# A two-layer encoder on one core: attention steps in another order, a rotation shared between VectorE and GpSimd, the low-part matmuls last, and a start with three panels

## The reference

```
h   = rmsnorm(x);  proj = h @ w_in            # 2048 x 4352, columns for A, B, C
A: 8 heads, attention with clipped relative bias, QK-norm
B: 16 query heads on 2 KV heads, window of 2 chunks, sinks, QK-norm + rotary
C: 4 heads, two softmax maps, p0 - lam * p1, QK-norm + rotary, then rmsnorm
x   = x + concat(A, B, C) @ w_out             # 2048 x 2048
x   = x + relu(rmsnorm(x) @ w_up)^2 @ w_down  # 2048 x 8192, 8192 x 2048
```

## Time and profile before

| | |
|---|---|
| median of 3 runs | 2122.57 us (2121.98 to 2126.64) |
| the profiled execution | 2122.87 us, of which the span of instructions is 2121.0 us |
| TensorE matmuls busy | 98% of the span |
| VectorE, ScalarE, GpSimd busy | 60%, 48%, 9% |

### The profile page before, as it was taken

How to read it: one execution, slowest core, us unless ns; L and a number is a source line. 1 busy time by engine, 2 the same in 40 slices (tenths; PEclk the granted TensorE clock), 3 DMA queues, 4 the chain that set the end, 5 groups by cost and what they waited for, 6 DMA issues and landing times.

```text
span 2121.0 us, 26490 instructions
## 1 busy us (share of the span) xinstructions
PE 2084.7 (98%) x10598; PEld 1738.0 (82%) x10598; DVE 1274.8 (60%) x1635; ACT 1010.3 (48%) x1353; POOL 197.6 (9%) x205
## 2 busy tenths in 40 slices
PE   7999999999999999999999999999999999999999
PEld 6877778888888888888878777788888888888887
DVE  6667556565565555556666675556655555565666
ACT  5456654443443444344445576544434434443444
POOL 2544120000000000000033431000000000000000
PEclk9999999999999999999999999999999999999999
DMA  8566786666666666666666568766666666666664
GB/s 262 163 183 169 178 230 178 189 189 195 190 189 191 191 189 195 190 189 190 185 175 181 159 177 204 202 182 187 194 192 189 190 196 190 189 190 194 189 192 149
DMA packets 209387, 400.70 MB, mean 189 GB/s; under 512 B 14862, under 2 KB 21872, under 8 KB 209264
## 3 DMA queue, kind: packets, MB, share of 16 engines
q1 hardware_dynamic: 203856, 381.85, 60.8%
q0 software_dynamic: 4608, 16.78, 4.3%
q10 hardware_dynamic: 800, 0.37, 0.1%
HBM read 380.05 MB, written 2.12 MB: 180 GB/s over the span
## 4 chain that ended last, share of the span: by engine, by line
PE 94%; DVE 2%; ACT 2%; issue 1%; DMA 1%; SPq 0%; DVEq 0%; POOL 0%; ACTq 0%; POOLq 0%
PE psum L475 22%; PE psum L439 19%; PE psum L441 19%; PE psum L440 18%; PE psum L478 12%; PE psum L485 1%; PE psum L545 1%; ACT w_hi L637 1%; DMA x<-in_x_dram 1%; PE psum L532 1%; PE psum L530 1%; DVE w_lo L806 1%; PE psum L571 0%; DVE probs L952 0%; DMA w_lo<-raw_ring 0%
## 5 line engine op out<-in xcount | busy, mean ns | idle before, releaser
L806 DVE TENSOR_TENSOR w_lo<-raw_ring,w_hi 128x1024 fp32r<-128x1024 f32 (+1 forms) x692 | 854.4, 1235 | 764.5 <-ACT w_hi L637 764.2
L637 ACT CAST w_hi<-raw_ring 128x1024 fp32r<-128x1024 f32 (+1 forms) x724 | 753.8, 1041 | 1006.5 <-PE psum L441 611.6
L475 PE MATMUL psum<-xt,w_hi 128*128 128x512 f32 x2048 | 512.9, 392 | 0.0
L439 PE MATMUL psum<-w_hi,ht_hi 128*128 128x512 f32 x1280 | 502.8, 393 | 1.3 <-DMA w_lo<-raw_ring 1.2
L441 PE MATMUL psum<-w_hi,ht_lo 128*128 128x512 f32 x1280 | 498.6, 390 | 0.0
L440 PE MATMUL psum<-w_lo,ht_hi 128*128 128x512 f32 x1280 | 498.3, 389 | 0.0
L475 PEld LDWEIGHTS psum<-xt,w_hi 128*128 128x128 f32 x2048 | 368.8, 189 | 66.3
L478 PEld LDWEIGHTS psum<-xt,w_lo 128*128 128x128 f32 x2048 | 279.4, 190 | 20.0
L478 PE MATMUL psum<-xt,w_lo 128*128 128x256 f32 x2048 | 285.6, 282 | 0.0
L439 PEld LDWEIGHTS psum<-w_hi,ht_hi 128*128 128x128 f32 x1280 | 240.3, 188 | 53.3 <-issue 5.1
L441 PEld LDWEIGHTS psum<-w_hi,ht_lo 128*128 128x128 f32 x1280 | 240.2, 188 | 50.8
(11 more groups left out here) (125 smaller groups left out, 1070.8 us busy)
## 6 DMA issues: line engine op xcount, KB each, us to landing
raw_ring<-in_w_up_dram SPq DMA_DIRECT2D x256, 512.0 KB, 3.7
raw_ring<-in_w_down_dram SPq DMA_DIRECT2D x256, 512.0 KB, 3.7
raw_ring<-in_w_in_dram SPq DMA_DIRECT2D x132, 512.0 KB, 4.2
raw_ring<-in_w_out_dram SPq DMA_DIRECT2D x64, 512.0 KB, 4.8
w_lo<-raw_ring POOLq DMA_DIRECT2D x32, 512.0 KB, 5.5
raw_ring<-in_w_in_dram SPq DMA_DIRECT2D x16, 256.0 KB, 2.8
x<-in_x_dram SPq DMA_DIRECT2D x4, 512.0 KB, 10.1
out_dram<-x SPq DMA_DIRECT2D x4, 512.0 KB, 3.9
```

What stands on the lines that cost most here:

```text
L439: pe.matmul(out_ap, t_hi, m_hi, start=start, stop=False, skip_group_check=True)
L475: pe.matmul(bank[:, f, :], w_hi[:, w, j, f * P:(f + 1) * P], both, start=kt == 0, stop=False, skip_group_check=True)
L637: act.copy(w_hi[:, u % AHEAD, :, 0:cols], raw_ring[:, u % RAWS, :, 0:cols]).then_inc(hi_ready, 1)
L806: dve.tensor_tensor(w_lo[:, u % AHEAD, :, 0:cols], raw_ring[:, u % RAWS, :, 0:cols], w_hi[:, u % AHEAD, :, 0:cols].bitcast(F32), ALU.subtr ...
```

## The change

What it does, part by part:

1. **Order in a rows unit.** The four tiles' hi·hi and lo·hi matmuls come first (8), then the four hi·lo ones. The wait for `w_hi` stands ahead of the 8, the wait for `w_lo` ahead of the last 4.
2. **Attention steps.** Both exponentials of a pair are in one step of ScalarE (s + 1), behind the split. `COMBINE` and `WEIGHT` are one step earlier on VectorE. `NORM_AT` has a table of its own: every head norm is one to four steps ahead of its old place. `POST_C` 0 goes from the front of step 46 to its end.
3. **Rotation.** Row tile 1 of Cq and Ck is rotated by VectorE (`rope`), right after their sums.
4. **Adding DMAs.** `SUMMED_UNITS` ends at 81: 14 units.
5. **x2 panels** (of the MLP's input) are two steps apart instead of one.
6. **Start.** Three panels before unit 0, panels 3 and 4 behind units 0 and 1; 10 and 14 further transposes of the identity (`warm`) into a PSUM bank that nobody reads. ScalarE issues its eight small DMAs after the second panel and its squares; SP issues the tables in step 3, and the parameters are worked out in steps 5 to 7.
7. **End.** In the last layer the unused panels, loads and splits are left out. The last unit does row tile 0 first, and each row tile is added and stored by itself.

```diff
-SUMMED_UNITS = list(range(55, 87, 2))
+SUMMED_UNITS = list(range(55, 83, 2))
-EXPS = {s + 1 + m: 2 * n + m for s, n in PAIR_AT.items() for m in range(2)}
-COMBINE = {s + 4: n for s, n in PAIR_AT.items() if n < 4}
-WEIGHT = {s + 3: n for s, n in PAIR_AT.items() if n >= 4}
+EXPS = {s + 1: n for s, n in PAIR_AT.items()}
+COMBINE = {s + 3: n for s, n in PAIR_AT.items() if n < 4}
+WEIGHT = {s + 2: n for s, n in PAIR_AT.items() if n >= 4}
-        T_USE[OUT_LAST[_c] + 2 + _n + (1 if _c == 1 else 0)] = ("x2", 2 * _c + _n)
+        T_USE[OUT_LAST[_c] + 2 + 2 * _n + (3 if _c == 1 else 0)] = ("x2", 2 * _c + _n)
-NORM_AT = {s: use[1:] for s, use in T_USE.items() if use[0] == "qk"}
+NORM_AT = {11: (0, 1), 13: (0, 0), 20: (1, 1), 22: (1, 0), 38: (3, 0), 45: (4, 0), 46: (4, 1), 52: (5, 0), 54: (5, 1),
+           58: (6, 0), 60: (6, 1), 66: (7, 0), 68: (7, 1)}
...
@@ block.tensor, rows_unit
-                unit_is_split(pl, u)
-                for j, kt in enumerate(kts):
-                    for r in range(RT):
-                        mm = three_passes(bank[r][:, 0:cols], src[0][:, kt, r * P:(r + 1) * P],
...
+                pe.wait_ge(hi_ready, pl.unit(u + 1))
+                final = pl.l == DEPTH - 1 and u == UNITS - 1
+                tiles = [(j, kt, r) for j, kt in enumerate(kts) for r in range(RT)]
+                for group in [[t for t in tiles if t[2] == r] for r in range(RT)] if final else [tiles]:
+                    for j, kt, r in group:
+                        for n, t in enumerate(src):
+                            pe.matmul(bank[r][:, 0:cols], t[:, kt, r * P:(r + 1) * P], w_hi[:, slot, j, 0:cols],
+                                      start=first and j == 0 and n == 0, stop=False, skip_group_check=True)
+                    unit_is_split(pl, u)
+                    for j, kt, r in group:
+                        mm = pe.matmul(bank[r][:, 0:cols], src[0][:, kt, r * P:(r + 1) * P], w_lo[:, slot, j, 0:cols],
+                                       start=False, stop=last and j == 1, skip_group_check=True)
+                    if final and r == 0:
+                        mm.then_inc(row0_done, 1)
                 mm.then_inc(unit_done, 1)
...
@@ block.tensor, start
+                if pl.l == 0 and s < 2:
+                    first_panel(3 + s)
...
-            for k in range(PANELS_BEFORE):
-                pe.wait_ge(x_loaded[k // 2], 16)
-                transposes(x_panel(k), start_banks[k])
+            warm(10)
+            first_panel(0)
+            first_panel(1)
+            warm(14)
+            first_panel(2)
...
@@ block.scalar
-                if s in EXPS:
-                    exponentials(pl, EXPS[s])
                 split_hi(pl, u, PROJ[u // UPC][2] if u < PU else CW)
...
+                if s in EXPS:
+                    for m in range(2):
+                        exponentials(pl, 2 * EXPS[s] + m)
...
+                if n == 1:
+                    load_small()
...
@@ block.vector
+            def rope(pl, c):
+                t, heads, half, r = c, 8, HD // 2, 1
...
+                dve.wait_ge(rope_ready, pl.l + 1)
+                dve.wait_ge(summed, pl.at(len(QK), QK.index(c) + 1))
+                dve.tensor_tensor(b_r[:, :, lo], a_r[:, :, hi], table(rope_s, 0, half), ALU.mult)
+                link(dve.tensor_tensor(b_r[:, :, hi], a_r[:, :, lo], table(rope_s, half, half), ALU.mult))
+                link(dve.tensor_tensor(a_r, a_r, table(rope_c, 0, HD), ALU.mult))
+                dve.tensor_tensor(a_r[:, :, lo], a_r[:, :, lo], b_r[:, :, lo], ALU.subtract)
+                link(dve.tensor_tensor(a_r[:, :, hi], a_r[:, :, hi], b_r[:, :, hi], ALU.add))
...
-                if s in POST_C:
-                    post_c(pl, POST_C[s])
                 if s in WEIGHT:
                     weight(pl, WEIGHT[s])
+                if s in NORM_AT:
+                    head_norm(pl, *NORM_AT[s])
+                if s in POST_C and POST_C[s]:
+                    post_c(pl, POST_C[s])
                 if s in STATS_AT:
                     head_sums(pl, STATS_AT[s])
-                if s in NORM_AT:
-                    head_norm(pl, *NORM_AT[s])
+                    if STATS_AT[s] < 2:
+                        rope(pl, STATS_AT[s])
...
@@ block.gpsimd, rotation
-                for r in range(RT):
+                for r in range(1 if c < 2 else RT):
```

More of the change, by code:

```diff
@@ L224, in encoder @@
         roped = sem("roped")
+        rope_ready = sem("rope_ready")
         normed = sem("normed")
@@ L361, in mix @@
                 u = s + FIRST_LOADS
+                if pl.l == 0 and s == 3:
+                    load_tables()
                 if u < PU:
@@ L986, in mix @@
                     split_lo(pl, u, PROJ[u // UPC][2] if u < PU else CW)
-                if s == 0:
+                if pl.l == 0 and s == 5:
+                    tables()
+                if pl.l == 0 and s == 6:
+                    parameters()
+                if s == (7 if pl.l == 0 else 0):
                     dve.tensor_copy(cur[:, :], par[:, pl.l, :]).then_inc(cur_ready, 1)
@@ L1002, in mix @@
                     add_out(pl, s)
+                if s in POST_C and not POST_C[s]:
+                    post_c(pl, POST_C[s])
             def mlp(pl, s, part, buf, c, k, n):
-                if s - 1 in PANEL_NUMBER:
+                more = pl.l < DEPTH - 1 or s + AHEAD < UNITS
+                if s - 1 in PANEL_NUMBER and used(pl, s - 1):
                     panel_lo(pl, s - 1)
-                if s < UNITS - 1:
+                if s < UNITS - 1 and more:
                     split_lo(pl, s + AHEAD)
@@ L1014, in mlp @@
                         dve.wait_ge(rstd_ready, pl.at(2, 2))
-                    dve.wait_ge(unit_done, pl.unit(s + 1 + AHEAD))
+                    final = pl.l == DEPTH - 1 and s == UNITS - 1
+                    if not final:
+                        dve.wait_ge(unit_done, pl.unit(s + 1 + AHEAD))
                     dve.wait_ge(evicted[p], pl.evictions(n))
@@ L1018, in mlp @@
                         v = x[:, r, (c % 4) * CW:(c % 4 + 1) * CW]
+                        if final and r == 0:
+                            dve.wait_ge(row0_done, 1)
+                        if final and r == 1:
+                            last.then_inc(row0_out, 1)
+                            dve.wait_ge(unit_done, pl.unit(s + 1 + AHEAD))
                         last = dve.scalar_tensor_tensor(v, acc[:, 2 * p + r, :], rstd[:, 1, r:r + 1], v, ALU.mult, ALU.add)
                     last.then_inc(evicted[p], 1)
-                if s == UNITS - 1:
+                if s == UNITS - 1 and more:
                     split_lo(pl, s + AHEAD)
```

168 lines of the change are left out of this document (95 added, 73 removed).

## The result

| | before | after |
|---|---|---|
| median, runs on the same chip | 2124.61 us (4 runs) | 2095.73 us (4 runs, 2095.67 to 2096.25) |
| profiled execution; span | 2122.87; 2121.0 us | 2095.73; 2093.6 us |

The ratio is 0.9866 with a 95% interval of [0.9854, 0.9878]: faster, by 28.9 us on the medians, where 19.8 had been forecast from the terms.

The account below looks back on a forecast made before the run. TensorE, busy 98% of the span, was taken as the bound, so only its waits and needless work count. Attention 17.5, start -1.7 and end 4.0 sum to 19.8 us off 2122.87: 2103 us, range 2096 to 2114.

Parts of the forecast that it names:

- What bounds the kernel: Whole kernel: TensorE's matmuls are busy 98% of the span, so only its waits or needless work can be won.
- Start: First units up to the PSUM bank behind unit 3: bank empty at 32.5 us, 0.9 later; 1.7 us lost in all.
- The landing of the second unit: Second weight unit's load at the start: lands at 14.21 us, less 1.25 for ScalarE's 0.37 MB no longer ahead.
- The issues: ScalarE's eight small DMA issues at the start: now stand in its chain ahead of the bank and add 4.2 us.
- The clock: TensorE after the idle time at the start: granted clock lost in one of two cases, half of 1.7 us, 0.8.
- The rival for this outcome: Start is won: issues cost little or loads come sooner, no clock lost; 2.5 instead of -1.7, 2095 to 2099 us; 12%.
- The rule on issuing engines: DMAs of different issuers share 16 engines: ScalarE's issues at 16 us compete with weight loads and worsen the chain; unpriced.
- Attention: TensorE's 13 waits for norms, weights, copies and an adding DMA: 19.5 us gross, 17.5 taken, ends 9 and 20.5.
- The x2 panels: Panels of the MLP's input, two steps apart: no wait of any size there, 0 us, ends -1 and +1.
- The rule on the shared port pair: VectorE and GpSimd block each other at SBUF: their rotations would push each other back, losing part of the gain.
- the rival that had them collide: Waits half replaced: VectorE and GpSimd collide at Cq and Ck, or issues take 8 us; 2107 to 2111 us; 18%.
- Order in the unit, end: Rows units' same 12 matmuls reordered: 0 us, upper end 17; kernel's end, panels 2.8, last addition 0.7, DMA 0.5: 4.0 won.

## Why the prediction was right, and where it was off

The direction and the mechanism were right, and the size was 7.6 us of span too small, in two terms: 3.8 us in the start and 3.8 in attention. With that the time fell just below the stated range.

**What bounds the kernel: right.** The gains that the unit starts place are idle time, lost clock or needless work of TensorE. In the MLP stages, two thirds of the span, only 0.2 us were won, at panels.

**Start: the mis-sized term, and of the wrong sign.** Forecast -1.7, measured +2.1, from one trace of each kernel, with a scatter of up to 1.4. Forecast was a bank empty at 14.21 - 1.25 + 8.0 + 0.6 + 4.2 + 6.74 = 32.5; it is empty at 28.00. Its pieces:
- The landing of the second unit, 14.21 - 1.25 = 12.96: it was cast at 9.96. This is the step that failed. I counted the bytes of ScalarE's queue only, and those I had about right (at least 1.1 us measured). The change also put SP's own tables, gains and norm2_g behind the weight loads, and of them I said nothing but that they are issued in step 3. Measured by putting them back: 2.5 us for that landing, 2.71 us of waiting for the fifth unit's load, and 4.0 us at unit 5.
- The issues: 4.2 forecast, 2.9 in the chain. They take 3.45 us (11.67 to 15.12), of which 0.6 beside the squares; the third panel's cast starts 5.21 us after the second unit's instead of 2.33. That they stand in the chain was right: that cast waits 2.79 us.
- The rest of the chain, 8.0 + 0.6 + 6.74 = 15.34, was 18.04 - 2.9 = 15.1: right. But the 2 us left out of it were called "DMA and table work", and 1.43 of them are a wait for the fifth unit's load in the earlier trace rows. That it went was not argued; it went with SP's new order, and with the old one it is back, at 2.71 us.
- The clock: the forecast took half of 1.7 us. It was lost in full in the profiled execution, 4.06 - 2.72 = 1.3 us.

The rival for this outcome was named, at 12%, with its price of 2.5. Its "the loads come sooner" is what happened; its "no clock is lost" is not. "Against: the last took 1.03" looked at the issues, and the issues were not what decided. Of the signs named for a right forecast, one failed for the same reason: the transposes behind unit 3 came at 28.09, not at 31 to 34 us.

**The rule on issuing engines: borne out, and I weighed it at the wrong place.** In 8 to 12 us the weight loads run at these rates (last column GB/s), first the changed kernel, then the one with ScalarE's DMAs at the start:

```profile
8.00:12.00 4.00, 4.00 (x22) 3.86 (x21) 2.99 (x4) 3.97 (x7) 0.00 (x0) 1.00 1.06 394
```

```profile
8.00:12.00 4.00, 4.00 (x25) 3.35 (x24) 3.13 (x5) 2.39 (x3) 0.00 (x0) 1.00 0.96 268
```

ScalarE's queue in those 4 us is 430 packets with 0.19 MB, and takes 33.8% of the DMA engines' time, with 18% of the bytes (the loads move 0.88 MB beside it):

```profile
q10 hardware_dynamic: 430, 0.19, 33.8%
```

By the Trainium skill's "DMA: Bandwidth & Descriptors", section "Issuing engines are not separate DMA queues", DMAs of different issuers run on the same 16 engines and interleave. These rows agree: another issuer's DMAs take time from the loads, and by more than their bytes. The prediction applied this to the issues at 16 us, as a loss. In the changed kernel no cast up to the bank waits for a load, so no loss is seen there; what is seen is the gain of what no longer stands at 8 us.

**Attention: right in kind, 3.8 us too low, panels included.** The 17.5 came from 13 waits, 19.5 gross less 2.0 left. The unit starts give:
- Gross 23.9 us, the sum of all gains over single units. I had left out the small rows of the waits (L880 1.0, L917 0.5, L922 0.4, in 6 waits), 1.9 us of idle time and about 3 with what a wait costs on top.
- A wait costs more than 0.16 us beside its idle time: with 1.42, 2.00, 0.70 and 2.34 us idle, 1.64, 2.21, 0.94 and 2.55 us were won. It is 0.22 in front of transposes.
- The clock was worth 1.4 us, not 1.7, and is kept now.
- New waits take 4.2 us, where I had 2.0 for all that is left: two of 1.45 and one of 0.74, all for L982. The cause of the first two is not what I named as a danger (the combined exponentials) but the norm ahead of the copy; the third is a split slowed beside GpSimd's tables.
- The x2 panels, priced at 0 with +1 as an end, won 0.7 us in each layer, and the next layer's x panels 0.2. Without these panels attention won about 19.6, inside the ends of 9 and 20.5.

The prediction's "this, not the order, is what makes Cq's first norm early enough", on the 6.1 us less of GpSimd, is not shown: undoing both costs 6.2 us, but GpSimd was done in time in either kernel. "The wait for an adding DMA was at unit 85 of the second layer, which VectorE now splits" did not hold as a cause: given back to the adding DMA, that unit waits no more, since its w_lo matmuls come last.

**The rule on the shared port pair: a mixed answer, as before.** GpSimd and VectorE at Cq, in the changed kernel:

```profile
47.53 2.95 POOL L1209 TENSOR_TENSOR small<-small 128x16 f32<-128x16 f32 x1
50.46 1.00 POOL L1232 TENSOR_TENSOR head_sq<-head_in,rope_s 128x256 f32<-128x256 f32 x1
...
56.48 1.72 POOL L1236 TENSOR_TENSOR head_in<-head_in,head_sq 128x256 f32<-128x256 f32 x1
```

```profile
48.11 0.69 DVE L925 TENSOR_TENSOR head_in<-head_in,rope_c 128x512 f32<-128x512 f32 x1
...
54.14 1.77 DVE L945 TENSOR_TENSOR head_in<-head_in,small 128x512 f32<-128x512 f32 x1
```

VectorE's whole rotation, 47.26 to 49.60, lies beside the reciprocal root of GpSimd, and neither is slowed (2.95 against 2.91 us in the earlier trace rows; 0.69 for 512 columns, where an undisturbed norm takes 0.68). VectorE's norm beside GpSimd's rotation takes 1.77 instead of 0.68 us, and that rotation 7.7 us, where with splits alone beside it it took 6.1 before and 7.1 in the run with GpSimd's rotation whole. By the Trainium skill's "SBUF — State Buffer", section "SBUF: two separate sides", each should block the other for whole instructions: the rotation's rows agree, and so does the split of 3.00 us beside GpSimd's tables, the root's don't. The two rotations do not meet, because the root stands ahead of GpSimd's (49.60 and 50.46 us); the rival that had them collide (18%) did not come.

**Order in the unit, end: right.** 0 and 0.0; 4.0 and 2.6 + 1.4 = 4.0. The w_up row's 0.230 belongs to its narrow matmuls, as said.

## What to carry to other kernels

When DMAs are moved, write down for every queue what they no longer stand in front of; a few hundred small packets can delay a neighbouring 512 KB load more than their bytes say. Before pricing a removed wait, add up all rows of waits, the small ones too, and for each operation moved ahead on an engine name the one that now stands behind it: here Bq1's norm, for which nobody had waited, went ahead of a copy and cost 1.6 us a layer. When an engine gets less to do, ask what it now does earlier, and beside whom: here GpSimd's tables moved beside a split and cost 0.9 us. And look at the chain in front of a late bank: three edits to order at the start gave 4.7 us, more than the whole end of the change.

## What the runs showed of the hardware

- A 1.99 us wait of TensorE was followed by a granted clock of 0.64, one of 1.76 us at the same place of the other layer by 1.00; before the change 2.34 us had 0.57 behind it once and 1.00 once.
- The column of the granted clock doesn't show all slow stretches: without the warm-up unit 0's matmuls start some 0.45 us apart, twice the usual, while the column reads 1.00 for 8 to 12 us. What holds TensorE back there is open.
- A split of VectorE (two inputs in SBUF) took 3.00 us instead of 1.23 beside a row of GpSimd instructions of 128x64; in two runs a GpSimd instruction took 1.67 us there instead, and the split 1.42.
